# The mixer's gate projections beside the second scan and the sparse attention, and the attention's scores two steps ahead

## What is computed

```python
h = rmsnorm(x, norm_mix[layer])
proj = h @ w_in[layer]
q_nsa, kv_nsa, g_nsa, q_gla, k_gla, v_gla, lr_gla, r_gla, g_merge = split_in_proj(proj)
...
o_a = nsa_attention(q_a, k_cmp, v_cmp, kv[2], kv[3], kv[4], kv[5], gates_a)
...
o_b = gla_chunked(heads(q_gla * GLA_DK ** -0.5, GLA_DK), heads(k_gla, GLA_DK),
                  heads(v_gla, GLA_DV), heads(log_a, GLA_DK))
o_b = rmsnorm(o_b.transpose(0, 2, 1, 3).astype(x.dtype), gla_norm[layer])
o_b = (o_b * jax.nn.silu(r_gla.reshape(b, t_len, GLA_HEADS, GLA_DV))).reshape(b, t_len, GLA_V_COLS)
gate_a, gate_b = jnp.split(jax.nn.sigmoid(g_merge), 2, axis=-1)
merged = gate_a * (o_a @ w_up_nsa[layer]) + gate_b * (o_b @ w_up_gla[layer])
x = x + merged @ w_out[layer]
```

## Time and profile before

| | us |
|---|---|
| median of 3 runs | 1931.63 (1931.22 to 1934.51) |
| profiled execution | 1931.55 |
| its span | 1929.8 |
| first scan with ten jobs (81.6 to 150.8) | 69 |
| to the attention's first turn of P | 107 |
| the attention from there (to 372.9) | 115 |
| merging (372.9 to 459.9) | 87 |

### The profile page before, as it was taken

One profiled execution on the slowest core, in us unless ns is written; L12 is line 12 of the kernel. 1 busy time (PEld: TensorE's weight loads), 2 busy tenths in 40 slices (PEclk: granted clock), 3 DMA queues, 4 the chain that ended last, 5 costly groups with the idle time before them and its releaser, 6 DMA issues.

```text
span 1929.8 us, 24905 instructions
## 1 busy us (share of the span) xinstructions
PE 1833.6 (95%) x10060; PEld 1461.2 (76%) x10060; DVE 935.6 (48%) x1964; ACT 712.7 (37%) x1533; POOL 617.1 (32%) x296
## 2 busy tenths in 40 slices
PE   6998789999999999999999989989899999999997
PEld 5777666788888888889766778877777777786665
DVE  4457677521410111124767365765744233666665
ACT  4342344433422231234445324442243333245450
POOL 3332211145344344434221322222422323332122
PEclk9998789999999999999999999999999999999999
DMA  5221210135233233324222222222422322321211
GB/s 159 81 86 55 55 31 28 44 110 159 71 109 107 80 97 99 98 83 107 58 42 66 88 69 66 66 66 66 120 55 66 77 66 79 91 61 43 51 55 66
DMA packets 215171, 148.45 MB, mean 77 GB/s; under 512 B 51968, under 2 KB 197392, under 8 KB 215056
## 3 DMA queue, kind: packets, MB, share of 16 engines
q1 hardware_dynamic: 210160, 135.27, 25.2%
q10 hardware_dynamic: 4896, 11.60, 1.8%
HBM read 144.74 MB, written 2.10 MB: 76 GB/s over the span
## 4 chain that ended last, share of the span: by engine, by line
PE 75%; DVE 17%; ACT 5%; issue 1%; DMA 1%; POOL 0%; ACTq 0%; SPq 0%; DVEq 0%
PE PS L435 20%; PE PS L436 19%; PE PS L437 19%; PE PS L577 6%; PE PS L523 5%; PE PS L607 3%; DVE X L1455 1%; PE PS L737 1%; DVE X L1459 1%; ACT P L1075 1%; DVE XTl L1467 1%; DVE X L1473 1%; DVE ST L1482 1%; DVE sm L1920 1%; DVE P L1523 1%
## 5 line engine op out<-in xcount | busy, mean ns | idle before, releaser
L2017 POOL TENSOR_TENSOR Wl<-Wr,Wh 128x1024 fp32r<-128x1024 f32 (+5 forms) x292 | 616.9, 2126 | 1275.2 <-ACT Wh L1008 1274.9
L435 PE MATMUL PS<-XTl,Wh 128*128 128x512 f32 (+1 forms) x1096 | 416.6, 380 | 13.8 <-DVE XTl L1467 6.9
L436 PE MATMUL PS<-XTh,Wl 128*128 128x512 f32 (+1 forms) x1096 | 411.7, 376 | 0.0
L437 PE MATMUL PS<-XTh,Wh 128*128 128x512 f32 (+1 forms) x1096 | 411.1, 375 | 0.0
L1008 ACT CAST Wh<-Wr 128x1024 fp32r<-128x1024 f32 (+5 forms) x292 | 267.3, 937 | 187.3 <-PE PS L437 141.0
L435 PEld LDWEIGHTS PS<-XTl,Wh 128*128 128x128 f32 x1096 | 208.9, 191 | 60.8 <-issue 12.4
L437 PEld LDWEIGHTS PS<-XTh,Wh 128*128 128x128 f32 x1096 | 209.0, 191 | 36.8
L436 PEld LDWEIGHTS PS<-XTh,Wl 128*128 128x128 f32 x1096 | 209.2, 191 | 35.1
L435 PE MATMUL PS<-Wl,XTh 128*128 128x512 f32 (+2 forms) x608 | 228.5, 376 | 4.2 <-DVE XTl L1467 3.7
L437 PE MATMUL PS<-Wh,XTh 128*128 128x512 f32 (+2 forms) x608 | 225.4, 371 | 0.0
L436 PE MATMUL PS<-Wh,XTl 128*128 128x512 f32 (+2 forms) x608 | 225.3, 371 | 0.0
(11 more groups left out here) (309 smaller groups left out, 2436.9 us busy)
## 6 DMA issues: line engine op xcount, KB each, us to landing
Wr<-in_w_in SPq DMA_DIRECT2D x38, 512.0 KB, 3.8
Wr<-in_fox_w_in SPq DMA_DIRECT2D x32, 512.0 KB, 4.1
Wr<-in_w_ffn_gate SPq DMA_DIRECT2D x22, 512.0 KB, 3.9
Wr<-in_w_ffn_up SPq DMA_DIRECT2D x22, 512.0 KB, 3.8
Wr<-in_w_ffn_down SPq DMA_DIRECT2D x22, 512.0 KB, 3.6
Wr<-in_swa_w_in SPq DMA_DIRECT2D x20, 512.0 KB, 4.0
Wr<-in_mla_w_in SPq DMA_DIRECT2D x16, 512.0 KB, 4.2
Wr<-in_mla_w_out SPq DMA_DIRECT2D x16, 512.0 KB, 3.4
```

What stands on the lines that cost most here:

```text
L435: pe.matmul(o, l[0], r[1], start=start, stop=False)
L436: pe.matmul(o, l[1], r[0], start=False, stop=False)
L437: return pe.matmul(o, l[0], r[0], start=False, stop=stop)
L2017: raw.tensor_tensor(l[:, 0:m], r[:, 0:m], h[:, 0:m].bitcast(F), sub).then_inc(*weight_lo.next(i))
```

## The change

The 16 gate projections are m0 to m7 and n0 to n7 (before: gb). m0 to m3 now stand beside levels 4, 7, 8 and 9 of the second scan, m4 to m7 and n0 to n6 in the attention, n7 ahead of the merging. ACT copies their results out of PSUM (m into X, n into NB) and takes all tanhs in the merging. The jobs beside the scans are listed by hand; `scan` 1 stands before `sum` 0, `normed` 0 and `turned` 0 behind levels 0 and 1 of the second scan. The attention is ordered by `paced_steps`, as the mla and fox stages are: turn x, norm x + 1, score x + 2, value x; P has two buffers. KV is copied by ACT instead of DVE. The mask MC is fetched before the first scan. X is fetched again at f = 4 to 7 instead of at the odd f. `paced_steps` itself is unchanged, `pair_steps` is gone.

```diff
@@ -240,12 +194,13 @@
                 KC, VC = alloc(c1, "KC", [128, 32]), alloc(c1, "VC", [32, 2, 64])
+                MC = alloc(c1, "MC", [128, 2, NT, 32])
...
-                n_att = attention(c1, 1)
-                MC = alloc(c1, "MC", [128, 2, NT, 32])
+                n_att = attention(c1)
...
+                NB = [alloc(c1, "nb", [128, T]) for _ in range(7)]
...
         def GA(f):
-            return X[:, f // 2, HALVES[f % 2]]
+
+            return X[:, f % 4, :].rearrange("p (h d c) -> p d h c", h=2, d=2)[:, f // 4]
+
+        def GF(f):
+            return NB[f] if f < 7 else MG[1]
...
-        gla_steps = []
-        left = list(nsa_jobs)
-        points = [0]
-
-        def share():
-            points[0] += 1
-            while left and (len(nsa_jobs) - len(left)) * 22 < len(nsa_jobs) * points[0]:
-                gla_steps.append(("job", left.pop(0)))
-
+        gla_steps = [("scan", 0)]
+        beside = {0: ["gv0", "gv1", "gv2", "gv3", "q0", "q1", "q2", "q3", "qr kv0", "kv1"],
+                  1: ["kv2", "kv3", "qt ck", "kt cv", "m0", "ck0 ck8", "cv0 cv8", "ca m1", "cb m2", "co m3"]}
         for dp in range(2):
-            gla_steps.append(("scan", dp))
             for li in range(10):
                 gla_steps.append(("level", (dp, li)))
-                share()
-            while "gv3" in left:
-                gla_steps.append(("job", left.pop(0)))
+                gla_steps += [("job", name) for name in beside[dp][li].split()]
+                if (dp, li) in ((1, 0), (1, 1)):
+                    gla_steps.append(("turned" if li else "normed", 0))
+            if dp == 0:
+                gla_steps.append(("scan", 1))
             gla_steps.append(("sum", dp))
-            share()
-            while dp and left:
-                gla_steps.append(("job", left.pop(0)))
-            gla_steps.append(("normed", dp))
-            share()
-            if dp == 0:
-                gla_steps.append(("turned", dp))
-        nsa_steps = pair_steps(8, ["tail"] + [f"m{f}" for f in range(8)], 0, lambda p: [], lambda p: [])
+        gla_steps.append(("normed", 1))
+        nsa_steps = paced_steps(8, ["m4", "m5", "tail", "m6", "m7"] + [f"n{f}" for f in range(7)], [4, 1, 1, 1, 1, 1, 1, 1, 1],
+                                lambda p: [("need", f"m{4 + p}")] if p < 2 else [], lambda p: [])
...
@@ -692,6 +641,10 @@
+                elif name[0] in "mn":
+                    f = int(name[1])
+                    c = (2856 if name[0] == "m" else 3880) + 128 * f
+                    proj_T((name[0], f), w[:, :, c:c + 128], XT, mix_in, (by_act, (name[0], f)))
...
@@ -804,12 +751,12 @@
                 elif kind == "turn":
+                    if x == 7:
+                        c_turn(3)
                     turn("nsa", x, P)
...
+            nsa_job("n7")
             for f in range(8):
-                proj_T(("gb", f), w[:, :, 3880 + 128 * f:4008 + 128 * f], XT, mix_in, (by_act, ("gb", f)))
                 proj_T(("ua", f), [(wa[u][:, :, tile(f)], 0, 64 * u) for u in range(2)], OA, [by_dve.at("nsa_o", 3)], (by_dve, ("ua", f)))
...
@@ -1144,14 +1096,17 @@
+            act.dma_start(MC[:, :, :, :], A["cmask"].rearrange("p (u i n) -> p u i n", u=2, i=NT)).then_inc(*mask_in.next("all"))
...
+                            elif name == "kv3":
+                                high(KV[:, i, :], bank["kv", i][:, :], "kv", i)
...
+                elif name[0] == "m":
+                    f = int(name[1])
+                    e.wait_ge(by_dve.at("on", f // 4))
+                    after(psum_full, "m", f)
+                    high(GA(f), split(bank["m", f][:, :]), "m", f)
+                elif name[0] == "n":
+                    f = int(name[1])
+                    after(psum_full, "n", f)
+                    high(NB[f][:, :], bank["n", f][:, :], "n", f)
...
@@ -1235,28 +1196,38 @@
+            def tanhs(f):
+                e.wait_ge(by_act.at("m", f))
+                act.activation(GA(f), GA(f), ACT.Tanh, scale=0.5).then_inc(*by_act.next("ga", f))
+                if f < 7:
+                    e.wait_ge(by_act.at("n", f))
+                    act.activation(NB[f][:, :], NB[f][:, :], ACT.Tanh, scale=0.5).then_inc(*by_act.next("gb", f))
+                else:
+                    after(psum_full, "n", 7)
+                    act.activation(MG[1][:, :], bank["n", 7][:, :], ACT.Tanh, scale=0.5).then_inc(*by_act.next("n", 7))
+
+            tanhs(0)
+            tanhs(7)
             for f in range(8):
-                s = f % 2
-                after(psum_full, "gb", f)
-                if f >= 2:
-                    e.wait_ge(by_dve.at("mt", f - 2))
-                act.activation(MG[2 * s + 1][:, :], bank["gb", f][:, :], ACT.Tanh, scale=0.5).then_inc(*by_act.next("gb", f))
+                if f < 6:
+                    tanhs(f + 1)
                 weights(psum_full, "ub", f)
...
@@ -1601,9 +1572,7 @@
                 elif name == "kv3":
-                    for i in range(NT):
-                        e.wait_ge(psum_full.at("kv", i))
-                        copy(KV[:, i, :], bank["kv", i][:, :], "kv", i)
+                    e.wait_ge(by_act.at("kv", 3))
```

More of the change, by code:

```diff
@@ L98, in wait_ge @@
                 self.seen[sem.name] = value
-def pair_steps(n, jobs, started, score, value, after=lambda p: [], gates=False, spread=7):
-    left, steps, waiting = list(jobs[started:]), [], []
-    total = len(left)
-    def run():
-        steps.append(("job", left.pop(0)))
-    def before(these):
-        for kind, x in these:
-            if kind != "need":
-                steps.append((kind, x))
-            while kind == "need" and x in left:
-                run()
-    def fill(p):
-        while left and (total - len(left)) * (spread + 1) < total * (p + 2):
-            run()
-    before(score(0))
-    steps.append(("score", 0))
-    steps.append(("norm", 0))
-    before(after(0))
-    fill(-1)
-    for p in range(n):
-        steps.append(("turn", p))
-        if p + 1 < n:
-            before(score(p + 1))
-            steps.append(("score", p + 1))
-        before(value(p))
-        steps.append(("value", p))
-        if gates:
-            before([("need", f"g{p}")])
-            steps.append(("gate", p))
-            waiting.append(p)
-        if p + 1 < n:
-            steps.append(("norm", p + 1))
-            before(after(p + 1))
-        fill(p)
-        for _ in range(8 if p == n - 1 else 2):
-            if waiting and not left:
-                steps.append(("out", waiting.pop(0)))
-    return steps
 def paced_steps(n, jobs, slots, score, value, after=lambda p: [], gates=False):
@@ L247, in program @@
                     GQ, GK = new("GQ", [128, 2, T]), new("GK", [128, 2, T])
-                    LR, GW2, BC = new("LR", [16, T]), new("W2", [16, 256]), new("BC", [128, 2])
+                    BC = new("BC", [128, 2])
                     MK = new("MK", [128, 8, 128])
@@ L805, in tensor @@
                         ob[0] = take(("nsa_o", a))
-                    elif a == 3:
-                        c_turn(3)
                     e.wait_ge(*free(ob[0]))
@@ L1146, in scalar @@
                 act.dma_start(CW2[j][:, :], A[f"cmp_{nm}_w2"][0]).then_inc(*cmp_in[j].next("all"))
+            act.dma_start(MC[:, :, :, :], A["cmask"].rearrange("p (u i n) -> p u i n", u=2, i=NT)).then_inc(*mask_in.next("all"))
             def nsa_job(name):
-                if name[-1].isdigit() and name[:-1] in ("gv", "q"):
+                if name[-1].isdigit() and name[:-1] in ("gv", "q", "kv"):
                     if name[-1] == "3":
@@ L1224, in scalar @@
                     else:
-                        f = int(x[1])
-                        after(psum_full, "m", f)
-                        act.activation(GA(f), bank["m", f][:, :], ACT.Tanh, scale=0.5).then_inc(*by_act.next("m", f))
+                        nsa_job(x)
                 elif kind == "score":
@@ L1240, in scalar @@
                     a = x // 2
-                    if a == 3:
-                        c_turn(3)
                     after(values_full, "nsa", x)
```

32 lines of the change are left out of this document (14 added, 18 removed).

## The result

The changed kernel takes 1910.88 us (median of 4 runs, 1910.16 to 1911.96); the kernel before, run beside it, takes 1933.04 (1931.22 to 1934.51). The ratio is 0.9886, with a 95% interval from 0.9869 to 0.9903: 22 us faster. The prediction was 1902.5, range 1895 to 1912. The sign and the range held, but the gain is 22 us where 29 were forecast, and the time lies close to the range's upper end.

The account below looks back on a forecast made before the run. The second scan was taken as bound by VectorE's chain, attention and merging by TensorE. Sum's end 245.0 + 26 + 110.8 = 381.8, plus merging 49.0 = 430.8 against 459.9: 29.1 us less, 1902.5 us, range 1895 to 1912.

Parts of the forecast that it names:

- MEMSET of DG: Start of the second scan on DVE: can start when TensorE's first sum is done, at 155.4 us in the trace.
- Normalisation in the chain: First output's normalisation, now between levels 0 and 1 of the second scan: adds 9.0 us to DVE's chain.
- Rotation and low part: kv3's rotation, the low part of OB and a wait for ACT, between levels 1 and 2: adds 6.5 us.
- Levels, 47.0 us carried over from before: Second scan, DVE from MEMSET of DG to Z of level 6: 47.0 us as before, blocked products kept.
- The third rival: Second scan: GpSimd's extra subtractions block DVE's chain, +9 to +12 us, so 1911.5 to 1914.5; chance 0.10.
- TensorE's 11 us of waiting: Second scan: DVE sets the time, TensorE waits for Z about 11 us, all of it before level 7.
- From Z of level 6 to the sum's end: End of second scan: 25.9 us of TensorE work plus 1.2 for a 1.2 GHz stretch, sum ending at 245.0.
- Start of the attention, 26 us: From the second sum's end to the first turn of P: 26 us, with a wait of 1.2 before m6.
- Attention's steps: From the first turn of P to the attention's end: 15.3 and 14.3 us a step, 110.8 in all.
- rival 2: Attention: values wait for the compressed scores' bank, 1.7 us in three steps, 1.0 in the first: 1908.5; chance 0.15.
- Merging: n7, then eight times ua and ub, TensorE-bound: 49.0 us instead of 87.0, ending at 430.8.
- rival 4: Merging: weights become the bound, 10.1 us a step instead of 5.44, +37 us: 1939.5; chance 0.04.

Follow-up runs that it names:

- e6: Changed kernel with the first output's normalisation and turn back between the two scans, ahead of the second scan's level 0: 1907.45 us.
- e7: Changed kernel with GpSimd writing zeros instead of subtracting for eleven weight pieces, kv3 to m3, beside the second scan (low halves left out): 1905.62 us.
- e10: Changed kernel with GpSimd's subtractions of weight pieces 20 to 36 cut into parts of 256 columns, whole computation kept: 1903.36 us.
- e9: Changed kernel with projection kv3 ahead of level 1 of the second scan on TensorE alone, ACT and DVE order unchanged: 1910.68 us.
- e12: e11 plus the first output's normalisation and turn between the scans with kv2 beside, and m0 and m1 one place earlier: 1899.98 us.
- e11: e10 plus m6 put ahead of the second pair's scores and the second output's turn: 1903.02 us.
- e1: Changed kernel with kv3 and its rotation ahead of level 1 of the second scan instead of behind it: 1915.38 us.

## Why the prediction was right, and where it was 8 us off

By its own steps:

- **MEMSET of DG**: forecast 155.4, came at 156.44 (+1.0; the first sum ended at 156.2, 0.8 later, where 0.5 either way had been allowed).
- **Normalisation in the chain**: forecast 9.0, took 9.7 (161.65 to 171.36; +0.7). Right in size. What I didn't ask was whether moving it buys anything: in e6 it doesn't.
- **Rotation and low part**: forecast 6.5, took 5.9 (-0.6), 2.32 of it the wait for ACT's copies.
- **Levels, 47.0 us carried over from before**: took 51.2 (+4.2). This is the step that failed, "I keep them as they are". The blocked products' excess rose from 8.4 to 14.9 us, 6.5 more (the prediction read 8 with two large ones; before has three, of 2.1 to 2.2). The 2.3 by which the chain grew less came back in VectorE's own waits, 7.4 us in this chain before and 4.9 after, above all those for a level's product on TensorE (4.3, now 0.9). The third rival had the mechanism, at 9 to 12 us; e7 and e10 show it. Z of level 6 came at 223.19, outside the 215 to 221 named, and the sign "levels 1 to 6 cost more than 66 us" was met (67.0 after the first sum), even though the total held.
- **TensorE's 11 us of waiting, "all of it before level 7"**: 10.7 us, and all before level 7, but 6.4 of it for a bank and not for Z. I missed the bank (kv0 to kv3 hold four). In e9, without the wait for the bank, the time is the same, so this omission didn't move the forecast.
- **From Z of level 6 to the sum's end**: forecast 27.1, took 25.6 (-1.5). The 1.2 us for a slow stretch didn't come; TensorE's clock is 1.00 there. The sum ends at 248.8 instead of 245.0.
- **Start of the attention, 26 us**: took 31.5, the second mis-sized term. m6 waited 4.19 us instead of 1.2, and then m6 ran 7.9 us instead of 5.44, its start at the lower clock. So the sign "clock 1.00 from 250 on" was not met either: 0.89 from 248.76 to 280.26. The second pair's exponentials started at 271.08, since PC's product (2.44 us) and normalising of the first P (4.55 us) stood blocked by GpSimd in VectorE's queue. I had carried normalising's gain (2.5 us) into the steps and not its full cost into the start. That PC's block counts, e10 supports (m6's wait fell to 2.4 us with PC's product at 0.83); for the normalising it is argued from the trace alone.

```profile
255.86 2.44 DVE L1709 TENSOR_TENSOR PC<-PC,MC 128x248 f32<-128x248 f32 x1
...
264.42 4.55 DVE L1494 TENSOR_SCALAR P<-P,sm 128x128 f32<-128x128 f32 x8
```

And m6 on TensorE, with its wait (its first three matmuls start 0.56 and 0.43 us apart, where 0.23 is the rule at the full clock):

```profile
272.14 0.77 PE L385 MATMUL PS<-XTl,Wh 128*128 128x512 f32 x1 [4.19 <-ACT P L1027]
272.70 0.63 PE L386 MATMUL PS<-XTh,Wl 128*128 128x512 f32 x1
273.13 0.63 PE L387 MATMUL PS<-XTh,Wh 128*128 128x512 f32 x1
```

- **Attention's steps**: forecast 110.8, took 110.64. No value waits (rival 2 falls), normalising takes 2.46 us as in the mla stage.
- **Merging**: forecast 49.0, took 49.00; rival 4 falls, at a DMA share of 0.45.

Sum: +3.8 (scan) +5.5 (start) -0.2 (steps) = 9.1 us later than the forecast 430.8, so 439.9; the 1.4 us of the later stages leave the profiled time 7.7 above the forecast. The two terms that are TensorE's alone were exact to 0.2 us; both that went wrong are VectorE chains in which GpSimd's subtractions block products: shown by e7 and e10 for the scan, in part for the start.

## What to carry to other kernels

Work moved beside an engine's waits brings its neighbours along: each projection here brought a GpSimd subtraction that can block VectorE's chain, so list what the new neighbours share, and cut the long ones up (four parts in place of one gave 7.5 us). Taking away a profile's longest wait need not gain anything (6.4 us went in one run, TensorE waited elsewhere and the time stayed), and moving steps of one serial engine past each other gained nothing by itself. Price a start-up as its own chain, and not with the durations of the steady state behind it.

## What the runs showed of the hardware

VectorE's block lasts to the end of GpSimd's running instruction and not to the end of its queue: beside subtractions of 1024 columns a product of 0.42 us took 2.4 to 2.6, beside rows of four of 256 columns 0.94 to 0.97. It also held a TENSOR_SCALAR of eight columns (1.98 us for 0.17, in the changed kernel), and four TENSOR_TENSOR_SCANs beside such parts took 2.76 us for 1.37 (e12). Normalising the first P, eight instructions in a row, got hardly shorter through the split (4.35 us in e10 and 4.88 in e11 and e12, for 4.55); each of the eight may meet a part of its own, which I haven't parted from other causes. The clock after a wait is not told by the wait's length: level 5 ran at 2.4 GHz after 3.56 us (1.16 us of product) in the changed kernel and at 1.2 GHz after 3.56 us (2.08 us) with kv3 moved (e1).
